# Eight-group modulation of a two-layer block: 16 pieces beside the input projection and 24 in the attention, instead of 32 and 8

## The reference, cut to what matters

```python
for layer in range(DEPTH):
    m = jnp.split((sc @ ada_w[layer] + ada_b[layer])[:, None, :], 6, axis=-1)
    mc = jnp.split(scc @ ada_w[layer] + ada_b[layer], 6, axis=-1)
    h = modulate(rmsnorm(x, nw[0]), m[0], m[1])
    hc = modulate(rmsnorm(xc, nw[0]), mc[0], mc[1])
    y, yc = even_mixer(h, hc, ...)
    x = x + m[2] * rmsnorm(y, nw[1])
    x = x + m[5] * rmsnorm(ffn(modulate(rmsnorm(x, nw[2]), m[3], m[4])), nw[3])
```

## Time and profile before

| | us |
|---|---|
| median of 3 runs | 2326.8 |
| lowest, highest | 2324.69, 2331.09 |
| profiled execution, its own time | 2330.8 |
| its span | 2329.0 |
| PE busy | 2121.9 (91% of the span) |
| DVE busy | 1446.8 (62%) |
| ACT busy | 1122.9 (48%) |
| POOL busy | 207.4 (9%) |
| DMA traffic | 507.17 MB, mean 218 GB/s |
| input projection of layer 0, first to last PE matmul | 51 to 265 |
| attention by pairs | 266 to 335 |

### The profile page before, as it was taken

The page is one execution under the profiler, slowest core; times in us unless marked ns, Lnnn a source line. Parts: engine busy times, 40 slices in busy tenths (PEclk is TensorE's granted clock), DMA queues, the critical chain, the costliest instruction groups (busy, mean ns, idle before and its releaser), DMA issues. The chain is left out here.

```text
span 2329.0 us, 27861 instructions
## 1 busy us (share of the span) xinstructions
PE 2121.9 (91%) x11070; PEld 1729.3 (74%) x11070; DVE 1446.8 (62%) x1437; ACT 1122.9 (48%) x1254; POOL 207.4 (9%) x219
## 2 busy tenths in 40 slices
PE   3999888998799999989667799999999999999994
PEld 2667467998588888878356678877788787878873
DVE  3652375336642232361667488888888888889884
ACT  3221252220532222351244477777777777777773
POOL 0100103224100000010631100000000000000001
PEclk8999999999899999999788799999999999999997
DMA  8576410000347332321003599999999999999994
GB/s 312 218 274 259 155 55 17 1 1 1 109 154 243 109 92 89 127 80 48 1 1 109 205 346 376 376 357 368 372 364 375 366 376 369 376 370 364 379 353 161
DMA packets 246378, 507.17 MB, mean 218 GB/s; under 512 B 11999, under 2 KB 80792, under 8 KB 239848
## 3 DMA queue, kind: packets, MB, share of 16 engines
q1 hardware_dynamic: 242791, 491.17, 58.8%
q0 software_dynamic: 3456, 14.16, 1.6%
HBM read 485.34 MB, written 19.96 MB: 217 GB/s over the span
## 5 line engine op out<-in xcount | busy, mean ns | idle before, releaser
L134 DVE TENSOR_TENSOR arena_r<-arena,arena_r 128x2048 fp32r<-128x2048 f32 (+2 forms) x456 | 927.8, 2048 | 344.2 <-ACT arena_r L130 343.3
L130 ACT ACTIVATE arena_r<-arena 128x2048 fp32r<-128x2048 f32 (+2 forms) x456 | 778.7, 1722 | 329.1 <-DMA arena<-in_moe_w 244.3
L2395 PE MATMUL bank<-arena_r,gate_rows_r 128*128 128x512 f32 x896 | 351.6, 392 | 0.0
L139 PE MATMUL bank<-hT_r,arena_r 128*128 128x512 f32 (+2 forms) x688 | 262.8, 382 | 15.2 <-DVE arena_r L134 12.6
L2393 PE MATMUL bank<-arena_r,arena_r 128*128 128x512 f32 x672 | 267.3, 398 | 0.2 <-DVE arena_r L134 0.2
L2394 PE MATMUL bank<-arena_r,arena_r 128*128 128x512 f32 x672 | 261.7, 389 | 0.0
L140 PE MATMUL bank<-catT_r,arena_r 128*128 128x512 f32 (+2 forms) x688 | 260.5, 379 | 0.0
L141 PE MATMUL bank<-hT_r,arena_r 128*128 128x512 f32 (+2 forms) x688 | 260.3, 378 | 0.0
L2395 PEld LDWEIGHTS bank<-arena_r,gate_rows_r 128*128 128x128 f32 x896 | 169.5, 189 | 36.6
L2424 PE MATMUL bank<-arena_r,hT_r 128*128 128x512 f32 x448 | 178.9, 399 | 16.8 <-DVE catT_r L2517 16.6
L2426 PE MATMUL bank<-arena_r,catT_r 128*128 128x512 f32 x448 | 175.3, 391 | 0.0
(11 more groups left out here) (376 smaller groups left out, 3061.2 us busy)
## 6 DMA issues: line engine op xcount, KB each, us to landing
arena<-in_moe_w SPq DMA_DIRECT2D x336, 1024.0 KB, 6.1
gate_rows<-in_ada_w SPq DMA_DIRECT2D x40, 1024.0 KB, 7.6
arena<-in_ffn_w SPq DMA_DIRECT2D x44, 512.0 KB, 5.2
arena<-in_ev_w_in SPq DMA_DIRECT2D x14, 1024.0 KB, 5.5
arena<-in_ffn_w SPq DMA_DIRECT2D x11, 1024.0 KB, 4.8
arena<-in_od_w_in SPq DMA_DIRECT2D x9, 1024.0 KB, 5.4
arena<-in_ada_w SPq DMA_DIRECT2D x8, 1024.0 KB, 17.4
expert_rows_in<-ada_bias_rows SPq DMA_DIRECT2D x8, 1024.0 KB, 7.2
```

The source lines that it names most:

```text
L130: return act.activation(rounded(hi), v, ACT.Copy)
L134: return dve.tensor_tensor(rounded(v), v, rounded(hi).bitcast(F32), ALU.subtract)
L139: pe.matmul(acc, xh_, wh_, start=start, stop=False)
L2395: mm = pe.matmul(out_bank, lo, wh[:, k, :], start=False, stop=(kk == KD - 1))
```

## The change

The table of the projection is halved: chunks 1 to 4 and 7 to 10 carry two pieces each, 16 in all (groups 1 and 2), and chunks 5, 6, 11 and 12 the closing steps. In the projection the pieces now stand ahead of the wait for the chunk's split weights (`s_il`) rather than behind it. The attention takes 24 pieces (groups 3, 4 and 5), and each pair runs two steps: pairs 0 to 3 take two pieces each, pair 4 holds all closing steps of the first group, pairs 5 to 8 and 9, and pairs 10 to 13 and 14, repeat that.

```diff
-        SLOTS_OF = (3, 3, 2)
...
-        IN_STAGE, IN_TURN = {3: 1, 6: 2, 9: 3, 12: 4}, {4: 1, 7: 2, 10: 3, 13: 4}
+        IN_SLOTS = {p: (2 * i, 2 * i + 1) for i, p in enumerate((1, 2, 3, 4, 7, 8, 9, 10))}
+        IN_STAGE, IN_TURN = {5: 1, 11: 2}, {6: 1, 12: 2}
...
         def ada_pe_beside(pe, it):
             n, d = divmod(it, n_group_jobs)
-            if n < 1 and d < KD:
-                ada_slot(pe, KD * (n + 4) + d)
-            elif n < 1 and d == n_group_jobs - 1:
-                ada_turn(pe, n + 5)
+            if n < 3 and d < KD:
+                ada_slot(pe, KD * (n + 2) + d)
+            elif n < 3 and d == n_group_jobs - 1:
+                ada_turn(pe, n + 3)
...
         def ada_sp_beside(sp):
-            for m in range(35, n_deferred):
+            for m in range(19, n_deferred):
...
+                        for n in IN_SLOTS.get(p, ()):
+                            ada_slot(pe, n)
                         if p in IN_TURN:
                             ada_turn(pe, IN_TURN[p])
                         pe.wait_ge(s_il, p + 1)
-                    if m == (p in IN_TURN):
-                        for n in IN_SLOTS.get(p, ()):
-                            ada_slot(pe, n)
...
-                pe.wait_ge(s_am, 5)
+                pe.wait_ge(s_am, 3)
...
-                  lambda dve, j: (gates_dve(dve, j), ada_dve_beside(dve, j)), bias_ready=(s_ncol, 4),
-                  pe_beside=ada_pe_beside, sp_beside=ada_sp_beside)
+                  lambda dve, i: (gates_dve(dve, i), ada_dve_beside(dve, 2 * i), ada_dve_beside(dve, 2 * i + 1)), bias_ready=(s_ncol, 4),
+                  pe_beside=lambda pe, i: (ada_pe_beside(pe, 2 * i), ada_pe_beside(pe, 2 * i + 1)), sp_beside=ada_sp_beside)
```

More of the change, by code:

```diff
@@ L249, in ada_close_group @@
                 ada_load_bias(sp, n + 1)
-        SLOTS_OF = (3, 3, 2)
-        IN_SLOTS = {p: tuple(range(8 * ((p - 1) // 3) + 3 * ((p - 1) % 3), 8 * ((p - 1) // 3) + 3 * ((p - 1) % 3) + SLOTS_OF[(p - 1) % 3]))
-                    for p in range(1, 13)}
-        IN_STAGE, IN_TURN = {3: 1, 6: 2, 9: 3, 12: 4}, {4: 1, 7: 2, 10: 3, 13: 4}
-        IN_LOADS = {p: tuple(m + 3 for m in IN_SLOTS[p]) for p in IN_SLOTS}
+        IN_SLOTS = {p: (2 * i, 2 * i + 1) for i, p in enumerate((1, 2, 3, 4, 7, 8, 9, 10))}
+        IN_STAGE, IN_TURN = {5: 1, 11: 2}, {6: 1, 12: 2}
+        IN_LOADS = {p: (2 * i + 3, 2 * i + 4) for i, p in enumerate((1, 2, 3, 4, 7, 8, 9, 10))}
         n_group_jobs = 10
@@ L259, in ada_pe_beside @@
             n, d = divmod(it, n_group_jobs)
-            if n < 1 and d < KD:
-                ada_slot(pe, KD * (n + 4) + d)
-            elif n < 1 and d == n_group_jobs - 1:
-                ada_turn(pe, n + 5)
+            if n < 3 and d < KD:
+                ada_slot(pe, KD * (n + 2) + d)
+            elif n < 3 and d == n_group_jobs - 1:
+                ada_turn(pe, n + 3)
         def ada_dve_beside(dve, it):
             n, d = divmod(it, n_group_jobs)
[L267 to L270, removed]
+            if n < 3 and d == n_group_jobs - 2:
+                ada_stage_rows(dve, n + 3)
+            elif n < 3 and d == n_group_jobs - 1:
+                ada_cols(dve, n + 3)
         def ada_sp_beside(sp):
-            for m in range(35, n_deferred):
+            for m in range(19, n_deferred):
                 ada_load_slot(sp, m)
@@ L595, in _ @@
                     ada_load_slot(sp, m)
-                for p in range(WCH - 1):
+                for p in range(WCH - NWR):
                     for m in IN_LOADS.get(p, ()):
                         ada_load_slot(sp, m)
[L599 to L604, removed]
+                    sp.wait_ge(s_pj, made[p])
+                    load_in(sp, p + NWR)
+                    if p == 6:
+                        ada_close_group(sp, 1)
+                ada_close_group(sp, 2)
             @block.gpsimd
@@ L743, in _ @@
                         ada_stage_rows(dve, IN_STAGE[p])
+                    if p in IN_TURN:
+                        ada_cols(dve, IN_TURN[p])
                     evacuate(dve, 1, s_pe_v, p)
-                    if p + 1 in IN_TURN:
-                        ada_cols(dve, IN_TURN[p + 1])
                     if p < PAIRS:
```

## The result

The changed kernel took 2343.2 us (median of 8 runs, 2336.34 to 2351.57) against 2326.7 for the kernel before (8 runs, 2324.69 to 2331.09). The ratio is 1.0072, 95% interval 1.0051 to 1.0092: slower by 0.7%, where 0.3% was forecast and 2342 was the end of the range. The direction and the places were right; the attention grew by more than I took.

What follows compares the result with a forecast made beforehand. PE, busy 91% of the span, was taken to bound the kernel. 2330.8 - 17.8 (projection) + 23.2 (attention) + 1.7 (clock) = 2337.9, or 2333.9 against the median; forecast 2334 us, range 2324 to 2342.

Steps and rivals of the forecast that it cites:

- the three kinds of wait: In the attention, PE was to wait for transfers, in the pairs' own steps, and for DVE's staging in the closing steps.
- the sum: Attention: +13.6 us until pair 10, +7.6 for pairs 10 to 13, +2.0 for pair 14, +23.2 in all; clock +1.7.
- The 17.8 us on the projection's side: Projection: 16.6 us saved by fewer pieces in the blocks and 1.2 by two turns fewer, -17.8 us.
- wait for the fourth piece: Early attention: PE stands from T = 4.7 until the fourth piece lands at T = 12.5, 7.8 us.
- waits for staging, pairs 4, 9, 14: Closing pairs of the attention: PE's turn waits for DVE's staging in the same pair, 2.3, 2.4 and 1.4 us.
- clock, beyond the steps: Attention: one more half-clock stretch than before among the waits of pairs 4 and 9, +1.7 us, bounds 0 and 5.
- The step that failed: Attention loads: buffer free after the piece three earlier plus 4.9 us; from pair 10, one needed every 3 us, delivered in 2.5.
- the paragraph on the closing steps: Pairs 4, 9, 14: PE waits for DVE's chain; loads queued behind in SP's queue add nothing.
- (a): Attention transfers slower than taken, 370 GB/s or 2.83 us a piece: +3.5 us, 2337.5 us; chance 0.17.
- (b): Attention: the clock falls at every new wait, four stretches more instead of one, 2339.4 us; chance 0.12.
- (c): Attention: not slower, second pieces fill PE's idle time, 2320.1 us, or 2327 if half is possible; chance 0.15.
- (d): Projection: PE runs into the split weights earlier, at most half of the 17.8 us lost, 2342 us; chance 0.06.

Runs made afterwards that it cites:

- the staging run: The changed kernel with DVE's staging of a group moved ahead of the maxima of its pair: 2335.5 us, ratio 1.0022 to the kernel before.
- the late table: The changed kernel with POOL's 2 MB bias table load held until 22 of the 40 deferred pieces are used: 2336.1 us, ratio 1.0022.

## Why the prediction was wrong

The direction and the three kinds of wait stood, the sum was 8.5 us short in the attention, and the missing part is in what it says on transfers. The 17.8 us on the projection's side came out to the tenth by luck: the projection gave 18.9, and it began 1.2 later for a reason that no run shows.

| step of the prediction | forecast | measured |
|---|---|---|
| first scores earlier | 17.8 | 17.8 (the projection itself 18.9, as it began 1.2 later) |
| wait for the fourth piece | 7.8 | 7.70, piece at T = 12.5 as said |
| its time at half clock, pair 2's pieces done | T = 18.7 | 19.3 |
| second piece of pair 3 done | T = 23.8 | 26.6 |
| waits for staging, pairs 4, 9, 14 | 2.3, 2.4, 1.4 | 2.10, 2.48, 1.45 |
| pair 10 starts | T = 53.8 | 60.4 |
| pairs 10 to 13 | 23.6, no wait for a transfer | 27.2, three of 1.29, 0.60 and 1.21 |
| pair 14 with its turn | 6.0 | 6.1 |
| clock, beyond the steps | +1.7 | one new stretch, in pairs 4 and 5, about +1 net |
| attention in all | 91.8 + 1.7 | 102.0 |
| behind it | nothing | nothing that the scatter lets see |

**The step that failed** is the one that begins "From there a load also needs its buffer, which is free when the piece three earlier is used, plus 4.9 us", with its conclusion "the queue delivers one in 2.5, so transfers are covered". The limit by buffers was right and its two sizes were wrong. The 4.9 us are the trip of a load with nothing ahead of it. With three buffers one or two loads are in flight ahead of nearly every load of this stage, and those took 5.3 to 8.7 us once the table was in; the median of all 21 is 7.3. The row had said so: its median of 7.6 stood beside the 4.8 that I took. The rate of 2.5 us a piece was read where the table and three loads were in flight; in pairs 5 to 8 the changed kernel's queue moved 364 GB/s, 2.9 us a piece.

With three buffers the second piece of a pair is loaded when the first piece of the pair before has been used, and PE wants it after one piece, a pair's own work and another piece: 0.9 + 1.8 + 1.0 = 3.7 us in a context pair and 5.9 in a latent one. Under a trip of 4.9 a latent pair is covered; the three that waited in pairs 11 to 13 had trips of 7.1, 7.9 and 7.8 us. The waits for pieces cost 2.8 us in pair 3, 4.2 in pairs 6 to 8 and 3.1 in pairs 11 to 13, 10.1 us where my steps had under 2. Of an attention of 93.5 us by the sum against 102.0, that is nearly all that was short. "A piece is needed every 3 us there and the queue delivers one in 2.5" compares two rates, and with three buffers the queue did not run at its own. The run with six buffers showed it: 424 GB/s in the second group, no wait in pairs 10 to 13, and waits for pieces of 6.7 us in all instead of 17.7.

The second miss is in the paragraph on the closing steps: "That holds back the 11th and 19th piece only, and both land about when they are needed". The 11th is the first of pair 6 and was 0.24 us late; the 19th is the first of pair 11 and was not late. But the staging run gained 3.4 us of waits for pieces beyond the 6.0, so the order in SP's queue may not be free either; that stays open.

Of the rivals, (a) named the rate that was measured: 364 GB/s in pairs 5 to 8 is within its 357 to 379. Its reason does not hold, since with six buffers the same group moved at 424; transfers were slower than I took because too few were in flight. The Trainium skill (DMA: Bandwidth & Descriptors, section Bandwidth) says that the HBM side, about 358 GB/s, binds for such loads, and also that its figure for a core alone is 425. This kernel runs on one core, and its 424 agree with the second and not with the first as a limit.

(b), the clock at every new wait, fell: of the three waits for the staging only the first was followed by half clock, which is the one stretch that the sum held. In the runs with six buffers and with the late table it was also the second, so the sum's one stretch more was partly luck. (c) fell in its sum, though a part of it was there: the second pieces covered 4.2 us of the waits for ACT and DVE. (d) fell: the projection gave all. Two of the rivals' times are off in the sum: (b) is 2333.9 + 5.1 = 2339.0 and not 2339.4, (d) 2342.8 and not 2342.

The case that I should have weighed is that one part of the change hurts by itself: two steps in a pair cost 8.5 us of attention even with eight pieces. The other part, more pieces at one step a pair, was not run: 16 pairs have no room for 24 pieces and their closing steps.

## What to carry to other kernels

A ring of n buffers is covered only if the work between the use of a buffer and the next need for it is longer than the trip from issue to landing. That trip is no constant: here it was 5 us for a load alone and up to 8.7 with two ahead, so neither the minimum nor the rate of a full queue stands for it, and a queue reaches its full rate only with enough loads in flight. The total must fit as well: two pieces wanted in 3.7 us are more than a queue can bring that takes 2.5 us for one, and buffers help there only by what they hold in advance. When work is moved from a stage in which transfers have slack to a shorter one, count bytes over the new stage's length and ask what else loads there; and when two steps that had other work between them fall into one, the one engine's wait for the other is the full chain of that step, unless the producer's part is moved to the front of it.

## What was not expected of the hardware

- The last part of a 1 MB load may land about 3 us after the bulk: the queue was down to 25 and 8 GB/s for 3 us while PE waited for the piece issued at 327.37 and had at 335.19.
- The same wait of 2.48 us of PE, for the staging of pair 9, was followed by a stretch of half clock in two kernels (six buffers, late table) and by none in the changed kernel. Such a stretch cannot be forecast from the length of a wait of this size.
- While POOL's mask runs (9.3 to 9.6 us), DVE's scalings beside it are slow, in every variant: two of them that take 0.35 us elsewhere took 1.64 and 2.24 in the kernel before, and each variant has one of over 2.2 us.
